# Feed forwards in 5 or 3 chunks of 4 to 8 hidden tiles instead of 2 chunks of 11, with a ring of three raw weight buffers and two modulation buffers

## The reference

```python
def swiglu(h, w_in, w_out):
    gate, up = jnp.split(h @ w_in, 2, axis=-1)
    return (jax.nn.silu(gate) * up) @ w_out
...
def conv_ffn(h, w_up, conv_w, w_down):
    up = h @ w_up
    a, b = up[..., :D_FF_2], up[..., D_FF_2:]
    return (jax.nn.silu(dwconv3(a, conv_w)) * b) @ w_down
...
        x = x + mx[2] * out_x
        x = x + mx[5] * swiglu(modulate(rms_norm(x, norm2_g[i]), mx[3], mx[4]), ffn_w_in[i], ffn_w_out[i])
        if need_ctx_out:
            y_ctx = y_ctx + mc[2] * out_c
            y_ctx = y_ctx + mc[5] * swiglu(modulate(rms_norm(y_ctx, norm2_g[i]), mc[3], mc[4]),
                                           ffn_w_in[i], ffn_w_out[i])
```

## Time and profile before

| | before |
|---|---|
| median of 3 runs | 3423.18 us (3422.95 to 3424.02) |
| span of the profiled execution | 3421.8 us |
| PE busy | 3319.9 us, 97%, 18320 matmuls |
| DVE busy | 1820.0 us, 53% |
| ACT busy | 1219.5 us, 36% |
| POOL busy | 235.9 us, 7% |
| read from HBM | 329.37 MB |

### The profile page before, as it was taken

The page is one execution under the profiler, slowest core; times in us unless marked ns, Lnnn a source line. Parts: engine busy times, 40 slices in busy tenths (PEclk is TensorE's granted clock), DMA queues, the critical chain, the costliest instruction groups (busy, mean ns, idle before and its releaser), DMA issues.

```text
span 3421.8 us, 43983 instructions
## 1 busy us (share of the span) xinstructions
PE 3319.9 (97%) x18320; PEld 2767.9 (81%) x18320; DVE 1820.0 (53%) x2870; ACT 1219.5 (36%) x1777; POOL 235.9 (7%) x336
## 2 busy tenths in 40 slices
PE   6998999999999999999999999999999999999999
PEld 4787788888888888878888887788888888678887
DVE  4677365334355454557667356476435445654344
ACT  4567332112234233343223335342122233543232
POOL 0001100000110000000003000100000110010001
PEclk9999999999999999999999999999999999999999
DMA  5500143324221212224544211143323222123232
GB/s 204 217 22 2 38 134 125 123 87 124 95 69 58 97 54 72 84 85 166 178 160 152 84 44 56 37 133 126 123 87 124 95 85 63 44 74 103 89 98 93
DMA packets 89463, 334.32 MB, mean 98 GB/s; under 512 B 10849, under 2 KB 15745, under 8 KB 85809
## 3 DMA queue, kind: packets, MB, share of 16 engines
q1 hardware_dynamic: 67856, 252.63, 21.9%
q0 software_dynamic: 21408, 78.88, 7.4%
HBM read 329.37 MB, written 2.10 MB: 97 GB/s over the span
## 4 chain that ended last, share of the span: by engine, by line
PE 88%; DVE 6%; ACT 4%; issue 1%; DMA 0%; POOL 0%; SPq 0%; ACTq 0%; DVEq 0%; POOLq 0%
PE PS L429 62%; PE PS L536 6%; PE PS L772 2%; PE PS L438 2%; PE PS L473 2%; PE PS L743 2%; PE PS L685 1%; PE PS L700 1%; PE PS L457 1%; PE PS L887 1%; PE PS L845 1%; PE PS L673 1%; DVE WL L1448 1%; PE PS L521 1%; DVE HL L1558 1%
## 5 line engine op out<-in xcount | busy, mean ns | idle before, releaser
L953 ACT ACTIVATE WH<-WR 128x1024 fp32r<-128x1024 f32 (+1 forms) x376 | 418.6, 1114 | 1381.7 <-PE PS L429 1191.3
L1448 DVE TENSOR_TENSOR WL<-WR,WH 128x1024 fp32r<-128x1024 f32 (+1 forms) x376 | 487.6, 1297 | 721.9 <-ACT WH L953 721.0
L429 PE MATMUL PS<-HH,WH 128*128 128x512 f32 (+1 forms) x2824 | 856.0, 357 | 12.8 <-DVE WL L1448 9.9
L429 PE MATMUL PS<-HH,WL 128*128 128x512 f32 (+1 forms) x2824 | 850.4, 355 | 0.0
L429 PE MATMUL PS<-HL,WH 128*128 128x512 f32 (+1 forms) x2824 | 848.8, 355 | 0.0
L429 PEld LDWEIGHTS PS<-HH,WH 128*128 128x128 f32 x2824 | 465.7, 188 | 101.8 <-DVE WL L1448 15.4
L429 PEld LDWEIGHTS PS<-HL,WH 128*128 128x128 f32 x2824 | 464.7, 188 | 79.6 <-issue 1.0
L429 PEld LDWEIGHTS PS<-HH,WL 128*128 128x128 f32 x2824 | 464.1, 188 | 78.4
L429 PE MATMUL PS<-DH,WH 128*128 128x512 f32 (+1 forms) x946 | 287.8, 357 | 0.0
L429 PE MATMUL PS<-DH,WL 128*128 128x512 f32 (+1 forms) x946 | 287.7, 357 | 0.0
L429 PE MATMUL PS<-DL,WH 128*128 128x512 f32 (+1 forms) x946 | 287.4, 357 | 0.0
(11 more groups left out here) (321 smaller groups left out, 4458.5 us busy)
## 6 DMA issues: line engine op xcount, KB each, us to landing
WR<-in_win SPq DMA_DIRECT2D x176, 512.0 KB, 3.5
AT<-in_adat POOLq DMA_DIRECT2D x144, 512.0 KB, 3.8
WR<-in_wdn SPq DMA_DIRECT2D x64, 704.0 KB, 4.1
WR<-in_wret SPq DMA_DIRECT2D x64, 512.0 KB, 3.2
WR<-in_zin SPq DMA_DIRECT2D x36, 512.0 KB, 3.4
AR<-in_ada SPq DMA_DIRECT2D x8, 1024.0 KB, 9.7
aV<-in_ada SPq DMA_DIRECT2D x8, 1024.0 KB, 4.9
aAR<-in_ada SPq DMA_DIRECT2D x8, 1024.0 KB, 6.5
```

Source lines behind the costliest of these rows:

```text
L429: mm = PE.matmul(dst[:, a:b], w[u % 2][:, k * P:(k + 1) * P], h[:, k, a:b], start=(k == 0 and i == 0), stop=(k == nk - 1 and i == 2))
L953: AC.activation(M.WH[u % 2][:, 0:n], M.WR[u % 2][:, 0:n], COPY).then_inc(*on.up("w_hi", u))
L1448: VE.tensor_tensor(M.WL[u % 2][:, 0:n], M.WR[u % 2][:, 0:n], M.WH[u % 2][:, 0:n].bitcast(F32), ALU.subtract).then_inc(*on.up("w_lo", u))
```

## The change

`CHUNKS` takes the place of `CH` and `FC`: layers 0 and 2 run chunks of 5, 5, 4, 4 and 4 hidden tiles, layers 1 and 3 chunks of 8, 7 and 7. Each chunk has its own 8 down units, so a layer has 40 or 24 of them instead of 16, each 5, 4, 8 or 7 k-tiles long. Raw buffers are three of 1024 columns, and a load waits for the low part of unit u-3; SP issues each load one place earlier in its program. WH and WL become one tile of 2048 columns each, which holds two units as before. The modulation tiles have two buffers instead of three, and a tile's last product with CB overwrites it. The memory of AT, D and the norm's tiles is laid out anew; the norms 0b and 2b have eight scaled tiles of their own. POOL issues CB and the modulation loads of layers 0 and 2 after the last HL of the norm before the feed forward. The context squares of layer 1 are made between modulation loads 8 to 15, and their norm tiles go beside four down units, two each, instead of two, four each. `HALVED` is empty: the branches for layers in it do nothing in this kernel.

```diff
-CH = 2
-FC = FT // CH
+CHUNKS = ((5, 5, 4, 4, 4), (8, 7, 7), (5, 5, 4, 4, 4), (8, 7, 7))
+LAST = [len(c) - 1 for c in CHUNKS]
+HALVED = ()
...
     def ffn(l):
-        for ch in range(CH):
-            add(("up", l, ch), f"win{l}", range(2 * ch * FC, 2 * (ch + 1) * FC), UNIT)
-            add(("down", l, ch), f"wdn{l}", range(ch * KT, (ch + 1) * KT), DUNIT)
+        for ch, nj in enumerate(CHUNKS[l]):
+            c0 = start(l, ch)
+            add(("up", l, ch), f"win{l}", range(2 * c0, 2 * (c0 + nj)), UNIT)
+            add(("down", l, ch), f"wdn{l}_{ch}", range(KT), nj * P)
...
-        self.WR = [t(f"WR{s}", [P, DUNIT]) for s in range(2)]
-        self.WH = [t(f"WH{s}", [P, DUNIT], F32R) for s in range(2)]
-        self.WL = [t(f"WL{s}", [P, DUNIT], F32R) for s in range(2)]
+        self.WR = [t(f"WR{s}", [P, UNIT]) for s in range(3)]
...
-                product(down + m, PS[m % 2 if m else 2], (M.DH, M.DL), FC, segs, after, ("d_lo", l, ch) if m == 0 else None,
-                        context_mean if l == 1 and ch and m == 1 else None)
...
+            for m in range(2 if l in HALVED else 0, KT if ch < LAST[l] or l == 1 else KT - 2):
+                product(down + m, PS[m % 2 if m else 2], D, nj, segs, after[m] if m < 3 else ("x_down", (l, ch, m - 2)),
+                        ("d_lo", l, ch) if m == 0 else None, context_mean if l == 1 and ch == LAST[l] and m == 1 else None)
         if l != 1:
-            product_tail(down + KT - 2, (M.DH, M.DL), FC, {0: "1a", 2: "3a", 3: "final"}[l],
-                         [("x_down", (l, 1, m)) for m in (KT - 4, KT - 3)])
+            product_tail(down + KT - 2, D, nj, {0: "1a", 2: "3a", 3: "final"}[l],
+                         [("x_down", (l, ch, m)) for m in (KT - 4, KT - 3)])
...
+    def modulation(l, n):
+
+        order = ada_order(l)
+        if n == 0:
+            PO.dma_start(flat(M.CB, 0, 2), dram["cb"][min(l // 2, 1)]).then_inc(*on.up("cb_load", l, 16))
+        if n >= NV:
+            return
+        if n > 1:
+            PO.wait_ge(*on("ada_taken", (l, order[n - 2])))
+        PO.dma_start(M.AT[n % 2][:, :], dram["adat"][l - 1, order[n]]).then_inc(*on.up(f"mod_load{n % 2}", (l, order[n]), 16))
...
+        if l not in HALVED:
+            PO.wait_ge(*on("h_lo", (f"{l}b", 1, KT - 1)))
+            for v in range(NV):
+                modulation(ada, v)
+            return
...
-        SP.dma_start(M.WR[u % 2][:, 0:n], dram[tensor][i]).then_inc(*on.up(f"load{u % 2}", u, 16))
...
+        SP.dma_start(M.WR[u % 3][:, 0:n], dram[tensor][i]).then_inc(*on.up(f"load{u % 3}", u, 16))
```

More of the change, by code:

```diff
@@ L62, in __call__, with start, plain, halves_order @@
         return self.handle(name), v
+def start(l, ch):
+    return sum(CHUNKS[l][:ch])
+def plain(l, ch):
+    return (2 if ch == 0 else 0) if l in HALVED else CHUNKS[l][ch]
+def halves_order(l, ch):
+    js = range(plain(l, ch), CHUNKS[l][ch])
+    out = []
+    for j in js:
+        if j == js[0]:
+            out += [(j, 1), (j, 2), (j, 6), (j, 7), (j, 5)]
+        elif j < js[-1]:
+            out += [(j, 1), (j - 1, 3), (j - 1, 4), (j, 6), (j, 7), (j, 2), (j, 5)]
+        else:
+            out += [(j, 1), (j - 1, 3), (j - 1, 4), (j, 6), (j, 7), (j, 5), (j, 2), (j, 4), (j, 3)]
+    return out
+def side(l, j, nj):
+    return (nj - 1 - j) % 2 if l in HALVED else 0
 def plan_units():
@@ L597, in feed_forward @@
         gate = "gate_taken" if l < 2 else "gate_taken_conv"
[L598 to L601, removed]
+        D = M.DH[l], M.DL[l]
+        for ch, nj in enumerate(CHUNKS[l]):
+            up, down, c0 = FIRST["up", l, ch], FIRST["down", l, ch], start(l, ch)
+            for j in range(plain(l, ch)):
+                jj = c0 + j
                 if j:
@@ new lines, in down_pair @@
+    def down_pair(l, ch, after):
+        u, nk, segs = FIRST["down", l, ch], CHUNKS[l][ch], segments(l)
+        for v, k0, k1 in ((0, 0, nk - 1), (1, 0, nk - 2), (0, nk - 1, nk), (1, nk - 2, nk)):
+            dst = PS[2 - v]
+            if k0 == 0:
+                PE.wait_ge(*on("w_lo", u + v))
+                PE.wait_ge(*on(*after[v]))
+            for k in range(k0, k1):
+                if v == 0:
+                    PE.wait_ge(*on("d_lo", (l, ch, k)))
+                for i, (w, h) in enumerate(((WH, M.DH[l]), (WH, M.DL[l]), (WL, M.DH[l]))):
+                    for a, b, _ in segs:
+                        mm = PE.matmul(dst[:, a:b], w(u + v)[:, k * P:(k + 1) * P], h[:, k, a:b],
+                                       start=(k == 0 and i == 0), stop=(k == nk - 1 and i == 2))
+            if k1 == nk:
+                mm.then_inc(*on.up("product", u + v))
@@ L1694, in feed_forward @@
         n = segs[-1][1]
-        SG, HF = M.WK[0], M.WK[1]
-        slots = ada_slots()
-        for ch in range(CH):
-            up, first = FIRST["up", l, ch], FIRST["down", l, ch]
-            for j in range(FC):
-                jj, u = ch * FC + j, up + 2 * j
-                refill(u + 2)
+        slots = ada_slots(ada) if ada is not None else {}
+        for ch, nj in enumerate(CHUNKS[l]):
+            up, first, c0 = FIRST["up", l, ch], FIRST["down", l, ch], start(l, ch)
+            for j in range(plain(l, ch)):
+                jj, u, s = c0 + j, up + 2 * j, side(l, j, nj)
+                SG, HF = M.WK[2 * s], M.WK[2 * s + 1]
+                refill(W.after(u, 2))
                 if l > 1:
@@ L2205, in pool_program @@
     squares("0b", T)
-    modulation(1)
-    PO.wait_ge(*on("d_lo", (0, 1, FC - 1)))
+    feed_forward(0, 1)
+    PO.wait_ge(*on("d_lo", (0, LAST[0], CHUNKS[0][-1] - 1)))
     squares("1a", T)
@@ L2210, in pool_program @@
     squares("1b", S)
-    modulation(2)
-    context_squares()
-    PO.wait_ge(*on("d_lo", (1, 1, FC - 1)))
+    for n in range(NV):
+        modulation(2, n)
+        if 8 <= n < 16:
+            context_square(n - 8)
+    PO.wait_ge(*on("d_lo", (1, LAST[1], CHUNKS[1][-1] - 1)))
     squares("2a", S)
```

678 lines of the change are left out of this document (533 added, 145 removed).

## The result

The changed kernel takes 3442.3 us (median of 4 runs, 3441.79 to 3442.95) where the kernel before took 3423.5 beside it: a ratio of 1.0060, interval 1.0048 to 1.0072. Forecast were 3445 us and a sum of +21.9; the profiled executions differ by 19.5 us (3421.8 and 3441.3). One of the 11 runs of best2, further down, took 11122 us at a granted clock of 0.46 and stands in no ratio.

The account below looks back on a forecast made before the run. PE, busy in 97% of the span, was taken to bound the kernel; losses 9.8 + 0.7 + 7.1 + 4.5 + 2.5 + 3.0 less gains 1.6, 0.3, 3.8 gave +21.9 and 3445 us, range 3431 to 3459.

Parts of the forecast that it names:

- chunk ends, layers 0 and 2: Where up turns to down, PE waits for D's last low part, 0.50 or 1.30 us, ten times: +9.8 us.
- chunk ends, layers 1 and 3: Same wait for D's last low part: 0 at chunks of 8, 0.18 us at chunks of 7, four times: +0.7 us.
- tail 1a, 3a, final: Norms after layers 0, 2 and 3: shorter split last units hide less of the norm chain, +7.1, +4.5, +2.5 us.
- clock behind the new stalls: After new stalls of 4 to 7 us PE's clock halves for a stretch, two counted: +3.0 us, bounds 0 and 10.
- third raw buffer: SP loads a unit one refill earlier, so the late weight load felt at 1157.79 us goes: -1.6 us.
- context squares: Layer 1's context squares no longer come in one block on POOL: -0.3 us.
- pace of later chunks: Twelve more up units per layer run at the second up stretch's faster matmul pace: -3.8 us.
- modulation buffers, CB, more units: Two AT buffers instead of three, CB loaded later, 64 more down units with DVE updates: no cost to PE.
- (d): Rival: clock falls after each of ten chunk ends, or CB comes late: 3459 us; chance 10%.
- (b): Rival: new buffer places quicken PE's pace between matmuls, making good the losses, 3411 us at 0.0045 us each; chance 5%.
- (c): Rival: chunk ends are hidden, so 9.8, the clock's 3.0 and half the tails fall out: 3425 to 3430 us; 8%.
- (e): Rival: the change does not do what it says; chance 2%.

Follow-up runs that it names:

- best2: Changed kernel with chunks of 7, 7 and 8 in all layers and each chunk's last tile ahead of the refill on DVE: 3420.1 us, ratio 0.9991.
- dfirst: Changed kernel with the last hidden tile of a chunk ahead of the last refill in DVE's program: 3430.8 us, ratio 1.0027.
- eleven2: Changed kernel with chunks of 11 and 11 in every layer and two raw buffers: 3420.6 us, ratio 1.0000 to the kernel before.
- c877: Changed kernel with layers 0 and 2 also in chunks of 8, 7 and 7: 3423.6 us, ratio 1.0009.
- last8: Changed kernel with layers 0 and 2 in chunks of 5, 5, 4 and 8: 3427.1 us, ratio 1.0009.
- ring2: Changed kernel with two raw buffers instead of three and each load in its old place: 3448.0 us, ratio 1.0076.
- swap: Kernel before with one weight load of the retention (head 1) moved ahead of the context tokens and distance table on SP: 3420.4 us, ratio 0.9989.
- pad16: swap with 16 more waits, on a signal long come, in PE's program ahead of layer 0's feed forward: 3419.7 us, ratio 0.9992.
- ring2swap: ring2 with the one weight load of retention head 1 ahead of the two tables: 3439.8 us, ratio 1.0048.
- pad8: swap with 8 more PE waits ahead of layer 0's feed forward and 24 ahead of layer 2's: ratio 0.9986.
- again: The changed kernel itself timed once more, nothing altered: 3442.7 us, ratio 1.0053 to the kernel before.
- ring2swapb: The same kernel as ring2swap, profiled a second time for its trace: 3441.6 us (one run).

## Why the prediction was right, point by point

| step | forecast | measured |
|---|---|---|
| chunk ends, layers 0 and 2 | +9.8 | +10.8 by the copies, -10.5 when taken away (dfirst) |
| chunk ends, layers 1 and 3 | +0.7 | +1.1 by the copies; 0.6 and 0.8 less in dfirst |
| tail 1a, 3a, final | +7.1, +4.5, +2.5 | +7.0, +4.4, +2.5 |
| clock behind the new stalls | +3.0 | about 0.25, within the +7.0 of 1a; +0.6 net in other places |
| third raw buffer | -1.6 | -1.6 of -3.4 in the retention, the rest clock |
| context squares | -0.3 | -0.3 (layer 1: +0.27 with 0.56 of chunk ends) |
| pace of later chunks | -3.8 | -1.9 in layer 0, -3.0 in layer 2, of which 1.1 was a draw |
| modulation buffers, CB, more units | 0 | 0 (eleven2, dfirst) |

**The chunk ends** were off by a tenth, with two errors against each other. The waits were forecast at 0.50 and 1.30 us, 9.8 in all, and came to 8.0; the overlap that each wait interrupts, 0.28 us ten times, was not in the sum. In layers 1 and 3 the same 0.28 is all that can be seen, four times, where the sum had 0.18.

**The tails** came out within 0.1 us. One reading was off: at 1a I had all of it ahead of the image part, and the trace shows the larger wait, 4.22 us, ahead of the context part, for WL. Both lie on the same DVE work, so the sum holds. The terms of 3a come to 5.6 + 5.96 + 4.2 = 15.8, not 15.6. In the trace the second one is 5.61 (from the update of X at 2798.86 to nTT at 2804.47), which makes 15.4.

**The clock** was the step that failed. Half clock stretches do come at the end of both large stalls:

```profile
1006.20:1009.60 3.40, 3.40 (x12) 2.37 (x11) 3.40 (x8) 2.89 (x5) 0.00 (x0) 0.51 0.42 152
2808.40:2811.80 3.40, 3.11 (x12) 2.96 (x13) 3.40 (x6) 1.03 (x2) 0.00 (x0) 0.50 0.47 154
```

But they cost little. At 3a PE lost time on the slower products, and its next wait gave that back: 15 us into the mixers it waits 0.80 us for WL, where it waited 1.36. PE before and PE in the changed kernel:

```profile
2818.20 0.50 PE L429 MATMUL PS<-HH,WH 128*128 128x512 f32 x1 [1.36 <-DVE WL L1448]
...
2834.41 0.50 PE L574 MATMUL PS<-HH,WH 128*128 128x512 f32 x1 [0.80 <-DVE WL L1775]
```

At 1a the means of the squares (L628) fall into the slow stretch, and the chain of the norm waits for them. From the update of X at 1007.40 to nTT at 1013.40 it takes 6.00 us, against 5.75 in c877 and last8, which have no slow stretch there, and 6.60 in ring2, where the stretch is twice as long. So some 0.25 us of the +7.0 is clock.

The +2.37 us ahead of the first feed forward, which I had not foreseen, holds three more stretches than before, the one at 70.9 us among them:

```profile
70.90:74.30 3.40, 3.40 (x10) 2.09 (x9) 0.00 (x0) 0.00 (x0) 0.00 (x0) 0.50 0.34 137
```

The change isn't needed for that: swap, pad16 and before are the same up to there, yet swap has 0.62 us and two stretches more and pad16 2.26 us more. Over all runs this part lies between -0.22 and +2.94. In the mixers of layer 3, alike in all these kernels, executions with two or three stretches stand within 0.3 us of before, those with one or none at -1.4 to -3.1. Of the 2.4 us between the forecast's sum and the spans, the clock in the tails was 3.0 too much and the pace 1.1 too little gain; the chunk ends (1.0 and 0.4) and the clock elsewhere (+2.4 at the start, -1.8 in the retention) stand against them, and a few tenths are left. That the sum came so close is in part luck: the clock at the start happened to cost about what was put down for the tails.

**The pace** of the first chunk of layer 2 is also luck. Before drew 8.48 us per unit there and the changed kernel 8.32, which is 1.1 us over its 7 units in that part; ring2swap, which drew 8.48, has +7.85 us in layer 2 instead of +6.77. Had before drawn 8.32 too, as pad16 and pad8 did (-3.03), the change would have gained nothing in layer 2.

**Rivals.** (d), a slow stretch after each chunk end, is out. The wait at 764.97 us ended at 766.09; the window behind it, and that behind the next chunk's:

```profile
766.10:776.10 10.00, 10.00 (x57) 8.88 (x58) 4.89 (x9) 1.55 (x3) 0.53 (x1) 1.00 0.36 107
867.30:877.30 10.00, 9.96 (x57) 8.85 (x58) 4.90 (x9) 1.50 (x3) 0.53 (x1) 1.00 0.34 106
```

A wait of 1.1 us between busy stretches leaves the clock at 1.00, and none of the 56 waits for D in the six traces that have them (after, again, ring2, ring2swap, ring2swapb, last8) is followed by a slow stretch. Each large wait at a tail was: 4.22 and 5.35 us here, 3.24 in c877, 2.55 in last8. Length alone doesn't settle it: the wait for the late load was 1.64 us in before, with no slow stretch behind it, and 1.79 in eleven2, with one. The Trainium skill (TensorE: Matmul & The Clock Gate, HAM oscillation) says that waits between bursts throttle the engine; in its example the waits are longer than the bursts. The traces agree for the tails. The chunk ends are short waits between long busy stretches, and there the prediction read more into the page than it says. (b) is out: the pace moved, but by 4.9 us where 3.8 were forecast. (c) is out by dfirst, which took the ten waits away and 10.5 us with them, and (e) by the order of the operations and the ten waits in the rows above.

## What to carry to other kernels

When a phase is cut into more pieces, price the drain at each end: the chain from the last product to the last operand, less what PE still has to do that doesn't need it. Work that stands in the same in-order engine ahead of that chain, and isn't urgent, belongs behind it; here three instructions in another order gave back about half of the loss. Cut so that the last piece is the large one if other work hides behind it. And before a buffer is added for a late load, look at what stands ahead of that load in its queue.

## What the runs showed of the hardware

PE's pace through the same program isn't fixed: 8.48 or 8.32 us for 48 products of 512 and 256 columns at full clock. In all 14 traces layer 0's first chunk ran at 8.48 and every chunk behind a down phase of layers 0 and 2 at 8.32; layer 2's first chunk ran at either, and one kernel showed both in two executions. What decides it is open. With the half clock stretches it makes executions of one kernel differ by some 3 us either way, more than the 1.6 us that swap was to show; only the ratio of many runs could tell that from nothing, and only just (0.9981 to 0.9998).
